# Constant products on TensorE in the waits of the router and of the last results, and a gather that begins with tile 0

## Chip, cores and metric

The kernel runs on one core of a Trainium2 chip. The metric is the device time of one execution in microseconds (us), and the median of several executions is compared.

## What is computed

A decoder trunk of two layers for one sequence of 256 tokens of width 1024, all float32. Each layer mixes tokens (layer 0 by causal pooling, layer 1 by attention with 16 heads), and then applies a mixture of experts: 32 experts in 4 groups, of which each token takes the best group and in it the best two experts. Cut to what matters here:

```python
for i in range(DEPTH):                                    # 2 layers
    h = rmsnorm(x, norm_mix_g[i]) * (1.0 + sc_m) + sh_m
    y = pool_mixer(...) if i % 2 == 0 else moba_attention(...)
    x = x + g_m * y
    h = rmsnorm(x, norm_ffn_g[i]) * (1.0 + sc_f) + sh_f
    x = x + g_f * hier_moe(h, ...)                        # 32 experts
return rmsnorm(x, final_norm_g)

# hier_moe: logits -> group, two experts e with weights combine[:, e]
for e in range(N_EXPERTS):
    he = jax.nn.silu(t @ w_gate[e]) * (t @ w_up[e])
    y = y + combine[:, e, None] * (he @ w_down[e])
```

sh, sc and g are six vectors per layer that come from the product of silu(c) with ada_w (1024 x 6144).

## The kernel before

The five engines run programs written out by hand, tied by semaphores. Nothing plans the order; what stands behind a waiting instruction on its engine waits too. SyncE (SP) issues all transfers of weights into `ring`, four slots of 3 MB (with a fifth slot `R` used once per layer), in a fixed order: an expert's gate and up weights are issued when its slot's `ring_free` comes (the slot's former gate and up have been used), its down weights at `down_free`.

The 256 tokens are two tiles (t = 0, 1) of 128. In each layer the mixture goes through these steps:

- `route(L)` on TensorE (PE): router logits, 16 transposes that bring x back to rows of tokens (line 557), the two small products of `strided`, and in layer 0 `part(7)`, a piece of silu(c) @ ada_w. Then it waits for `mask_ready`, the mask of chosen experts that VectorE (DVE) works out step by step. Five small products of 32 columns with the mask give the counts (`counts`), and `cols(7 + 8 * L)` does six products of one column each (128 x 1).
- From the counts DVE works out the place of each token among 512 places sorted by expert, and writes `pick[:, t, :]`, 128 x 512, of ones and zeros, in two instructions for each tile (lines 1542 and 1397; `pick_ready` rises after each tile).
- `gather(L)` on PE: for each of 8 blocks k of 128 features, two products over the tiles t into `bank[k % 4]` give the sorted tokens. It waits for both tiles of `pick`. ScalarE (ACT) moves each bank to `hS` (in `reg_a`, line 1094, `hS_ready`), and blocks 4 to 7 wait until the bank is free again.
- `first_hidden(L)` takes expert 0, then come the experts, 64 places each, in a rotation. Four times (`STAGES` and the end) `combine(L, s)` turns 128 finished places back to rows (8 transposes, line 726), waits until ACT and DVE have moved them to `yS` (line 1669 on DVE), and adds them into banks 4 to 7.
- `last_results(L)` ends the experts: the last transposes `turn_ye_of` (line 616), after which DVE writes the scaled result (line 1394), for which `combine(L, SB - 1)` waits.

All ordinary products stand at line 496 in the profile, in the helper `mm`. One float32 product of the program is two MATMUL instructions in the trace: a gather has 16 products and 32 instructions. In the names, `keep` holds `pick`, `reg_h` the tokens, `ye` the small arrays of the router, `cst` constants (the identity `ident` is its first 128 columns), `colp` and `colq` the vectors of the layer.

Of the kernel before, what the change touches and what calls it, by code (L numbers as in the profile page):

```python
# [11 lines left out]
T = SEQ // P  # L12
KC = D // P
NSLOT = SEQ * TOPK
SB = NSLOT // P
# [96 lines left out]
def program(nc, x, c, ada_w, ada_b, norm_mix_g, norm_ffn_g, pool_w, pool_scale, w_qkv, w_o,  # L112
# [3 lines left out]
    with ctx:  # L116
        def sb(name, shape, dt=F32):
            return ctx.enter_context(nc.sbuf_tensor(name, shape, dt))
# [3 lines left out]
        def S(*name):  # L122

            key = "_".join(map(str, name))
            if key not in sems:
                sems[key] = ctx.enter_context(nc.semaphore(key))
            return sems[key]
# [3 lines left out]
        cst = sb("cst", [P, NM])  # L131
        ident, tri = cst[:, 0:P], cst[:, P:2 * P]
# [47 lines left out]
        h_str = reg_h[:, :].rearrange("p (t k q) -> p t k q", t=T, k=KC)  # L180
# [3 lines left out]
        pick = keep[:, 0:T * NSLOT].rearrange("p (t s) -> p t s", t=T)  # L184
# [81 lines left out]
        bank = [ctx.enter_context(nc.psum_tensor(f"bank{i}", [P, 512], F32)) for i in range(8)]  # L266
# [10 lines left out]
        def cols_w(s, n):  # L277
            return ring[:, s, 0:KC * n].rearrange("p (k n) -> p k n", k=KC)
# [14 lines left out]
        def full_at(turn):  # L293

            return 16 * (turn + 1)
# [16 lines left out]
        def turn_bank(s, half):  # L312

            return bank[((STAGES + (0,))[s] + half) % 2]
# [17 lines left out]
        def lg_at(t, n):  # L332

            return bank[5][:, 384 + t * 64:384 + t * 64 + n]

        def cols_at(a):

            if a in (7, 15):
                return bank[4][:, 0:NB]
            return bank[7 if a < 8 else 6][:, NB * (a % 8):NB * (a % 8 + 1)]  # L340
# [153 lines left out]
        def _(pe):  # L494
            def mm(o_, l_, r_, start, stop):
                return nc.tensor.matmul(o_, l_, r_, start=start, stop=stop)  # L496

            def part(a, ready=None):

                s, turn = ADA_AT[a]  # L500
                w = cols_w(s, AC)
                if a:
                    pe.wait_ge(S("acc_act"), 2 * ADA_PE.index(a if ready is None else ready))
                for kk in range(2):
                    if kk == 0:
                        pe.wait_ge(S("ring_first", s), full_at(turn))
                    else:
                        pe.wait_ge(S("ring_mid", s), full_at(turn))
                        pe.wait_ge(S("ring_last", s), full_at(turn))
                    for b, (lo, hi) in enumerate(((0, 512), (512, AC))):  # L510
                        for g in range(4):
                            k = 4 * kk + g
                            last = mm(bank[part_bank[a][b]][32 * g:32 * g + 32, 0:hi - lo],
                                      cact[:, k:k + 1].broadcast_to([P, 32]), w[:, k, lo:hi], kk == 0, kk == 1)
                        if kk:
                            last.then_inc(S("part_full"), 1)

            def blocks(a, dst):

                one = quarter if a in ADA_PE else ones[:, 0:1]  # L520
                for j in range(NB):
                    if j in (0, 4):
                        pe.wait_ge(*acc_done(a, j // 4))
                    last = mm(dst[:, j:j + 1], acc_of(a)[:, j * P:(j + 1) * P], one, True, True)
                return last

            def cols(a):
                blocks(a, cols_at(a)).then_inc(S("cols_full"), 1)

            def strided(L):  # L530
# [3 lines left out]
                    last = mm(strided_at[:, i * KC:(i + 1) * KC], spread[:, i, :], in_eight, True, True)  # L534
                last.then_inc(S("strided_full"), 1)

            def squares(L, k):

                pe.wait_ge(S("sq_ready"), L * KC + max(k, 3) + 1)
                mm(bank[1][32 * (k % 4):32 * (k % 4) + 32, 0:SEQ], ones[:, 0:32], sqT[:, k, :], k < 4, k >= KC - 4)\  # L540
                    .then_inc(S("sums"), 1)
# [4 lines left out]
            def route(L):  # L546

                pe.wait_ge(S("L_kept"), L + 1)
                pe.wait_ge(S("S_kept"), L + 1)
                pe.wait_ge(S("bb_ready"), 1)  # L550
                for t in range(T):
                    mm(lg_at(t, NL), Lsb[:, t * P:(t + 1) * P], pull, True, True)
                    last = mm(lg_at(t, NL + 1)[:, NL:NL + 1], Ssb[:, t * P:(t + 1) * P], quarter, True, True)
                last.then_inc(S("lg_full"), 1)
                for t in range(T):
                    for k in range(KC):
                        last = nc.tensor.transpose(bank[2 * t + k // 4][:, k % 4 * P:(k % 4 + 1) * P],
                                                   xT[:, k, t * P:(t + 1) * P], ident)
                        if k % 4 == 3:
                            last.then_inc(S("x_back"), 1)  # L560
                pe.wait_ge(S("g_kept"), L + 1)
                strided(L)
                if L == 0:
                    part(7)
                pe.wait_ge(S("mask_ready"), L + 1)
                for t in range(T):
                    mm(bank[5][:, 0:E], ones[:, :], mask[:, t, :], t == 0, t == T - 1)
                mm(bank[5][:, E:2 * E], tri, mask[:, 0, :], True, True)
                mm(bank[5][:, 2 * E:3 * E], ones[:, :], mask[:, 0, :], True, False)
                mm(bank[5][:, 2 * E:3 * E], tri, mask[:, 1, :], False, True).then_inc(S("counts"), 1)  # L570
                cols(7 + 8 * L)

            def gather(L):

                pe.wait_ge(S("xr_ready"), 4 * L + 4)
                pe.wait_ge(S("x_kept"), 4 * L + 4)
                pe.wait_ge(S("pick_ready"), L * T + T)
                for k in range(KC):
                    if k >= 4:
                        pe.wait_ge(S("hS_ready"), L * KC + k - 3)  # L580
                    for t in range(T):
                        last = mm(bank[k % 4][:, :], h_str[:, t, k, :], pick[:, t, :], t == 0, t == T - 1)
                    last.then_inc(S("gathered"), 1)
# [71 lines left out]
            def turn_ye_of(L, e, b):  # L655

                pe.wait_ge(S("ye_ready", L), e + 1)
                turn_ye(bank[2 + b], b).then_inc(S("ye_turned", L), 1)
# [29 lines left out]
            def last_results(L):  # L688

                turn_ye_of(L, E - 2, 0)  # L690
                down_of(L, E - 1, *loaded(L, E - 1), 1)
                turn_ye_of(L, E - 1, 1)

            def overflow(L):

# [21 lines left out]
            def combine(L, s):  # L717

                if s == 0:
                    for half, t in by_tile:  # L720
                        mm(bank[4 + half + 2 * t][:, :], ident, x_sb[:, t, half * 512:half * 512 + 512], True, False)
                for half in range(2):
                    if half and s < SB - 1:
                        pe.wait_ge(S("heT_ready", L), STAGES[s] + 4)
                    for mq in range(4):
                        last = nc.tensor.transpose(turn_bank(s, half)[:, mq * P:(mq + 1) * P],  # L726
                                                   yT[:, half * 4 + mq, s * P:(s + 1) * P], ident)
                    last.then_inc(S("yT_turned"), 1)
                pe.wait_ge(S("yS_act"), SB * L + s + 1)
                pe.wait_ge(S("yS_dve"), SB * L + s + 1)  # L730
                for half, t in by_tile:
                    last = mm(bank[4 + half + 2 * t][:, :], pwT[:, s, t * P:(t + 1) * P],
                              yS[s][:, half * 512:half * 512 + 512], False, s == SB - 1)
                    if s == SB - 1:
                        last.then_inc(S("moe_out"), 1)
# [30 lines left out]
            for k in range(KC):  # L766
                for t in range(T):
                    last = nc.tensor.transpose(two(0, k)[:, t * P:(t + 1) * P], x_sb[:, t, k * P:(k + 1) * P], ident)  # L768
# [6 lines left out]
            for t in range(T):  # L775
                last = mm(bank[6][:, :], ones[:, :], band_sb[:, t, 0:2, :], t == 0, t == T - 1)
# [3 lines left out]
            for k in range(KC):  # L780
                for t in range(T):
                    last = mm(two(0, k), h[:, t, k * P:(k + 1) * P], band_sb[:, t, k // 2, :], t == 0, t == T - 1)
# [3 lines left out]
            for t in range(T):  # L786
                last = mm(bank[6][:, :], ones[:, :], band_sb[:, t, 2:4, :], t == 0, t == T - 1)
# [6 lines left out]
            for k in range(KC):  # L794
                pe.wait_ge(S("pT_ready"), 2 * (k // 2) + 2)
                for cc in range(2):
                    last = mm(mixed(0, k), pw[:, k // 2 * 2 + cc, k % 2 * P:(k % 2 + 1) * P], pT[:, k // 2 * 2 + cc, :],
                              cc == 0, cc == 1)
# [1092 lines left out]
```

## Time and profile before

| | |
|---|---|
| time, median of 3 (785.62, 787.03, 787.3) | 787.03 us |
| profiled execution: time, span | 786.15 us, 784.3 us |
| PE busy | 723.5 us, 92% of the span |
| DVE, ACT, POOL busy | 241.9, 170.1, 39.5 us |
| granted TensorE clock, mean | 0.972 |
| DMA, mean | 351 GB/s |

The profiled execution took 1.85 us more than the span from its first to its last instruction. PE is busy nearly throughout; its granted clock (PEclk) is 1.00 (2.4 GHz) or 0.50 (1.2 GHz). Times within the trace are from the start of the span.

### The profile page before, as it was taken

Reading aid. Unit: us, or ns where it says so; the run is one execution under the profiler, and the core shown is the slowest. Engines: PE = TensorE matmul, PEld = TensorE weight load, DVE = VectorE, ACT = ScalarE, POOL = GpSimd, SP = SyncE. Lnnn points to the kernel's source line nnn. Section 1 sums busy time; section 2 is a strip of 40 time slices with the busy share of each in tenths; the row PEclk is TensorE's granted clock in tenths of the full one; section 3 lists DMA queues with packets and bytes.
Section 4 is the critical chain, followed back from the end, with each engine's and each line's share of the span. In section 5 each row is a group of like instructions: output and inputs, shape, how many; then the busy total and the mean of one; then the engine's idle time right before and its main releaser. Section 6 shows DMA issues by size and latency. Waiting matters only on the chain.

```text
span 784.3 us, 12427 instructions
## 1 busy us (share of the span) xinstructions
PE 723.5 (92%) x4568; PEld 430.2 (55%) x4568; DVE 241.9 (31%) x660; ACT 170.1 (22%) x394; POOL 39.5 (5%) x71
## 2 busy tenths in 40 slices
PE   4988699999989999979999999969999998999995
PEld 2664545555544445426888888744555554454542
DVE  0113515111211211153777553261511221121113
ACT  4112441111110111142123232244111111011113
POOL 0000000000100000000000000000000100000000
PEclk9989799999999999997999999979999999999999
DMA  8999999999999999999796755182999999999961
GB/s 342 396 400 391 412 367 377 386 418 415 420 415 417 417 416 418 403 391 331 298 378 239 237 196 232 64 333 99 386 384 422 417 417 417 416 419 414 418 246 56
DMA packets 70451, 274.93 MB, mean 351 GB/s; under 512 B 4480, under 2 KB 17920, under 8 KB 53888
## 3 DMA queue, kind: packets, MB, share of 16 engines
q1 hardware_dynamic: 70400, 274.23, 88.3%
q8 instruction: 34, 0.56, 0.3%
q14 instruction: 17, 0.14, 0.0%
HBM read 273.16 MB, written 1.05 MB: 350 GB/s over the span
## 4 chain that ended last, share of the span: by engine, by line
PE 83%; DMA 9%; DVE 3%; issue 2%; SPq 1%; ACT 1%; DVEq 0%; ACTq 0%
PE bank L496 74%; DMA ring<-in_exp_w_up_dram 5%; PE bank L616 4%; DMA ring<-in_ada_w_dram 4%; PE bank L603 2%; PE bank L726 1%; SPq L361 1%; PE bank L909 1%; DVE ye L1394 1%; PE bank L768 0%; DVE keep L1397 0%; DVE reg_h L1669 0%; DVE keep L1669 0%; DVE reg_a L1397 0%; ACT ye L1049 0%
## 5 line engine op out<-in xcount | busy, mean ns | idle before, releaser
L496 PE MATMUL bank<-ring,xe 128*64 128x256 f32 x1984 | 227.8, 382 | 6.6 <-DMA ring<-in_exp_w_up_dram 6.1
L496 PEld LDWEIGHTS bank<-ring,xe 128*64 128x64 f32 x1984 | 139.6, 137 | 78.3 <-issue 12.1
L496 PE MATMUL bank<-ring,heT 128*64 128x512 f32 x512 | 123.9, 604 | 0.0
L1394 DVE TENSOR_TENSOR reg_c<-reg_c,bank 128x128 f32<-128x128 f32 x64 | 18.5, 288 | 279.6 <-ACT reg_c L1113 279.6
L468 POOL COPY xe<-reg_a 128x512 f32 x62 | 38.1, 614 | 689.0 <-PE bank L496 368.1
L1049 ACT ACTIVATE ye<-bank 128x512 f32<-128x512 f32 (+1 forms) x72 | 41.7, 585 | 139.1 <-PE bank L496 138.9
L1113 ACT ACTIVATE reg_c<-bank 128x128 f32<-128x128 f32 x64 | 17.8, 278 | 241.1 <-PE bank L496 238.6
L496 PE MATMUL bank<-reg_b,ring 128*128 128x256 f32 x256 | 60.9, 393 | 1.7 <-ACT reg_b L1258 1.7
L1394 DVE TENSOR_TENSOR reg_b<-bank,colp 128x512 f32 x64 | 44.3, 692 | 43.3 <-issue 35.8
L496 PEld LDWEIGHTS bank<-ring,heT 128*64 128x64 f32 x512 | 31.2, 136 | 47.3 <-issue 47.0
L496 PEld LDWEIGHTS bank<-reg_b,ring 128*128 128x128 f32 x256 | 49.5, 197 | 8.9 <-issue 2.2
L496 PE MATMUL bank<-ring,cact 128*32 128x512 f32 (+1 forms) x320 | 32.8, 548 | 19.5 <-DMA ring<-in_ada_w_dram 16.9
L616 PE MATMUL bank<-cst,ye 128*128 128x128 f32 x256 | 41.9, 286 | 2.9 <-ACT ye L1049 2.9
L1397 DVE SCALAR_TENSOR_TENSOR ring<-ring,cact 128x768 f32<-128x768 f32 x42 | 42.7, 1017 | 1.2
L616 PEld LDWEIGHTS bank<-cst,ye 128*128 128x128 f32 x256 | 26.7, 140 | 28.1 <-issue 23.1
L496 PE MATMUL bank<-reg_a,ring 128*128 128x256 f32 x160 | 39.2, 405 | 2.2 <-DVE reg_a L1397 1.5
L496 PE MATMUL bank<-keep,reg_h 128*128 128x512 f32 x64 | 33.6, 691 | 4.4 <-DVE keep L1397 4.4
L603 PEld LDWEIGHTS bank<-cst,reg_c 128*128 128x128 f32 x64 | 8.9, 138 | 50.5 <-issue 48.7
L496 PEld LDWEIGHTS bank<-reg_a,ring 128*128 128x128 f32 x160 | 32.0, 204 | 8.3 <-issue 2.1
L496 PEld LDWEIGHTS bank<-ring,cact 128*32 128x32 f32 x320 | 10.3, 118 | 39.2 <-issue 38.1
L1637 DVE COPY heT<-bank 128x128 f32<-128x128 f32 x64 | 18.7, 292 | 42.3 <-PE bank L603 42.3
L496 PE MATMUL bank<-ring,reg_b 128*128 128x256 f32 x128 | 29.8, 386 | 0.0
(165 smaller groups left out, 543.5 us busy)
## 6 DMA issues: line engine op xcount, KB each, us to landing
ring<-in_exp_w_gate_dram SPq DMA_DIRECT2D x64, 1024.0 KB, 13.6
ring<-in_exp_w_up_dram SPq DMA_DIRECT2D x64, 1024.0 KB, 15.6
ring<-in_exp_w_down_dram SPq DMA_DIRECT2D x64, 1024.0 KB, 12.7
ring<-in_ada_w_dram SPq DMA_DIRECT2D x16, 1536.0 KB, 12.3
ring<-in_ada_w_dram SPq DMA_DIRECT2D x32, 768.0 KB, 12.4
ring<-in_w_qkv_dram SPq DMA_DIRECT2D x12, 1024.0 KB, 12.3
ring<-in_w_o_dram SPq DMA_DIRECT2D x4, 768.0 KB, 7.5
x_sb<-in_x_dram SPq DMA_DIRECT2D x1, 1024.0 KB, 5.1
```

What stands on the lines that cost most here:

```text
L361: sp.dma_start(dst[:, a:b], src[:, a:b]).then_inc(S(name, s), 16)
L468: nc.gpsimd.tensor_copy(xe[:, b, :, :], hS[:, :, bass.ds(off, CAP)]).then_inc(S("xe_ready", L), 1)
L496: return nc.tensor.matmul(o_, l_, r_, start=start, stop=stop)
L603: return nc.tensor.transpose(dst[:, 2 * P:3 * P], he[:, b, :], ident)
L616: last = nc.tensor.transpose(dst[:, cq * P:(cq + 1) * P], ye[:, b, cq * P:(cq + 1) * P], ident)
L726: last = nc.tensor.transpose(turn_bank(s, half)[:, mq * P:(mq + 1) * P], yT[:, half * 4 + mq, s * P:(s + 1) * P], ident)
L909: last = nc.tensor.transpose(bank[5 + a][:, s * P:(s + 1) * P], sc[m % 2][a][:, s * P:(s + 1) * P], ident)
L1049: return nc.scalar.activation(o_, i_, ACT.Identity)
L1113: nc.scalar.activation(sil[:, b, :], bank[b][:, 0:P], ACT.Silu).then_inc(S("sil_ready", L), 1)
L1394: return nc.vector.tensor_tensor(o_, a_, b_, op)
L1397: return nc.vector.scalar_tensor_tensor(o_, a_, s_, b_, op0, op1)
L1637: nc.vector.tensor_copy(heT[:, b, :], bank[b][:, 2 * P:3 * P]).then_inc(S("heT_ready", L), 1)
```

## The change

A new helper `keep_busy(n, b)` on PE issues n products of the identity with the first 512 columns of `cst`, which never change, into bank b. Nothing reads their result. It is called in five kinds of places: in `route`, before the wait for the mask (4 products, layer 1 alone) and after `cols` (1 in layer 0, 3 in layer 1), at the end of `last_results` (1), and in the last `combine` between the transposes and the wait for `yS` (1). And `gather` does tile 0 of blocks 0 to 3 as soon as tile 0 of `pick` is there, then tile 1 of these blocks; blocks 4 to 7 are as before. No other engine's program is changed.

```diff
+            def keep_busy(n, b):
+
+                for i in range(n):
+                    mm(bank[b][:, :], ident, cst[:, 0:512], True, True)
+
...
                 strided(L)
                 if L == 0:
                     part(7)
+                else:
+                    keep_busy(4, 6)
                 pe.wait_ge(S("mask_ready"), L + 1)
...
                 cols(7 + 8 * L)
+                keep_busy(3 if L else 1, 6)
 
             def gather(L):
 
                 pe.wait_ge(S("xr_ready"), 4 * L + 4)
                 pe.wait_ge(S("x_kept"), 4 * L + 4)
-                pe.wait_ge(S("pick_ready"), L * T + T)
-                for k in range(KC):
-                    if k >= 4:
-                        pe.wait_ge(S("hS_ready"), L * KC + k - 3)
+                for t in range(T):
+                    pe.wait_ge(S("pick_ready"), L * T + t + 1)
+                    for k in range(4):
+                        last = mm(bank[k][:, :], h_str[:, t, k, :], pick[:, t, :], t == 0, t == T - 1)
+                        if t == T - 1:
+                            last.then_inc(S("gathered"), 1)
+                for k in range(4, KC):
+                    pe.wait_ge(S("hS_ready"), L * KC + k - 3)
                     for t in range(T):
                         last = mm(bank[k % 4][:, :], h_str[:, t, k, :], pick[:, t, :], t == 0, t == T - 1)
                     last.then_inc(S("gathered"), 1)
...
                 turn_ye_of(L, E - 1, 1)
+                keep_busy(1, 0)
...
                     last.then_inc(S("yT_turned"), 1)
+                if s == SB - 1:
+                    keep_busy(1, 2)
                 pe.wait_ge(S("yS_act"), SB * L + s + 1)
```

On PE in layer 0, between `cols(7)` (the products of 128x1) and the gather, the order with its waits changes so; `cst` alone is the constant product:

```order
 L496 MATMUL bank<-cst,ring 128x1 [waits acc_act]
 L496 MATMUL bank<-cst,ring 128x1
+L496 MATMUL bank<-cst 128x512
 L496 MATMUL bank<-keep,reg_h 128x512 [waits pick_ready,x_kept,xr_ready]
-L496 MATMUL bank<-keep,reg_h 128x512 x7
+L496 MATMUL bank<-keep,reg_h 128x512 x3
+L496 MATMUL bank<-keep,reg_h 128x512 [waits pick_ready]
+L496 MATMUL bank<-keep,reg_h 128x512 x3
 L496 MATMUL bank<-keep,reg_h 128x512 [waits hS_ready]
```

One product is put ahead of the gather, and the eight products of blocks 0 to 3 are split into four for tile 0 and four that wait for tile 1.

On PE in layer 1, from `strided` (128x8) to the products with the mask (`ye`), the order changes so:

```order
 L496 MATMUL bank<-cst,ring 128x8 [waits spread_ready,g_kept]
 L496 MATMUL bank<-cst,ring 128x8
+L496 MATMUL bank<-cst 128x512 x4
 L496 MATMUL bank<-ye,ones 128x32 [waits mask_ready]
 L496 MATMUL bank<-ye,ones 128x32
```

Four products stand ahead of the wait for the mask. Three more stand behind `cols(15)`, where layer 0 has one; the gather is split in the same way.

On PE at the end of a layer, from the last `turn_ye_of` (line 616, now 628) to the last products of `combine`:

```order
-L616 MATMUL bank<-cst,ye 128x128 [waits ye_ready_0]
-L616 MATMUL bank<-cst,ye 128x128 x3
-L752 COMPARE_AND_BRANCH [waits dn_free_0]
-L726 MATMUL bank<-cst,reg_b 128x128 x8
+L628 MATMUL bank<-cst,ye 128x128 [waits ye_ready_0]
+L628 MATMUL bank<-cst,ye 128x128 x3
+L496 MATMUL bank<-cst 128x512
+L767 COMPARE_AND_BRANCH [waits dn_free_0]
+L739 MATMUL bank<-cst,reg_b 128x128 x8
+L496 MATMUL bank<-cst 128x512
 L496 MATMUL bank<-reg_h,reg_c 128x512 [waits yS_dve,yS_act]
```

One product stands ahead of each of the two waits.

## Rows read from the trace of the kernel before

**Rows 1.** The page: the span, and PE's clock in 40 slices.

```profile
span 784.3 us, 12427 instructions
...
PEclk9989799999999999997999999979999999999999
```

**Rows 2.** Chain that ended last, in order of time: start, length (us), what.

```profile
93.51 0.75 DVE keep L1397
...
95.59 20.61 PE bank L496 x64
...
212.30 21.29 DMA ring<-in_exp_w_up_dram
...
524.39 0.75 DVE keep L1397
...
526.47 20.21 PE bank L496 x64
```

**Rows 3.** Windows: stretch, length, busy by engine (instructions), PEclk, DMA share, GB/s.

```profile
88.05:93.40 5.35, 5.34 (x30) 4.77 (x22) 2.21 (x10) 2.54 (x5) 0.00 (x0) 0.50 1.02 416
95.59:101.70 6.11, 6.11 (x8) 2.50 (x9) 4.86 (x13) 0.78 (x1) 0.00 (x0) 0.50 1.01 414
351.16:354.28 3.12, 3.12 (x20) 1.10 (x24) 2.69 (x6) 0.98 (x2) 0.00 (x0) 0.50 1.09 348
360.10:364.50 4.40, 4.14 (x38) 4.04 (x36) 0.17 (x1) 0.00 (x0) 0.00 (x0) 1.00 1.07 358
366.25:371.36 5.11, 5.11 (x12) 4.12 (x13) 0.80 (x3) 2.25 (x4) 0.00 (x0) 0.50 1.07 379
516.70:521.50 4.80, 1.09 (x11) 1.08 (x10) 3.27 (x22) 4.78 (x8) 0.00 (x0) 1.00 1.00 412
521.56:524.28 2.72, 2.72 (x14) 2.63 (x13) 2.21 (x10) 0.91 (x3) 0.00 (x0) 0.50 0.17 63
526.47:531.79 5.32, 5.32 (x7) 2.22 (x8) 4.79 (x13) 0.78 (x1) 0.00 (x0) 0.50 0.99 416
770.20:774.93 4.73, 1.77 (x15) 1.30 (x13) 1.39 (x2) 1.85 (x3) 0.00 (x0) 1.00 0.01 2
```

**Rows 4.** Timeline of weight loads in layer 0's gather: start, length, what.

```profile
96.58 0.34 PEld L496 LDWEIGHTS bank<-keep,reg_h 128*128 128x128 f32 x1 [0.52 <-issue]
...
100.84 0.34 PEld L496 LDWEIGHTS bank<-keep,reg_h 128*128 128x128 f32 x1 [0.52 <-issue]
...
102.14 0.19 PEld L496 LDWEIGHTS bank<-keep,reg_h 128*128 128x128 f32 x1 [0.24 <-issue]
...
111.58 0.19 PEld L496 LDWEIGHTS bank<-keep,reg_h 128*128 128x128 f32 x1 [0.24 <-issue]
```

**Rows 5.** Timeline: products of one column, a bank moved by ACT, the first hidden products.

```profile
57.60 1.47 PE L496 MATMUL bank<-cst,ring 128*128 128x1 f32 x12 [0.38 <-ACT ring L1049]
...
102.33 0.78 ACT L1094 ACTIVATE reg_a<-bank,colq 128x512 f32<-128x512 f32 x1 [2.11 <-PE bank L496]
...
112.53 3.67 PE L496 MATMUL bank<-ring,reg_a 128*64 128x256 f32 x32
...
521.58 2.70 PE L496 MATMUL bank<-ones,ring 128*128 128x1 f32 x12
...
543.01 3.67 PE L496 MATMUL bank<-ring,reg_a 128*64 128x256 f32 x32
```

**Rows 6.** Timeline of PE at the end of layer 1.

```profile
772.97 1.08 PE L726 MATMUL bank<-cst,reg_b 128*128 128x128 f32 x8 [0.99 <-DVE reg_b L1394]
...
774.93 3.67 PE L496 MATMUL bank<-reg_h,reg_c 128*128 128x512 f32 x8 [0.88 <-DVE reg_h L1669]
```

**Rows 7.** Windows again, for the DMA share; and a row of the waits.

```profile
114.00:119.00 5.00, 5.00 (x47) 3.32 (x45) 1.64 (x9) 2.44 (x5) 0.86 (x2) 1.00 0.52 179
...
534.00:546.00 12.00, 12.00 (x50) 5.76 (x50) 0.00 (x0) 6.15 (x8) 0.61 (x1) 1.00 0.00 0
...
PE bank L496 <- DMA ring<-in_exp_w_up_dram: 6.1, 5, 1.6
```

## The prediction

> **What bounds the kernel now.** I read the page first. The span is 784.3 us, and PE's clock is below 9 (90% of full speed) in only four of the 40 slices; two of these are the fifth (78 to 98 us) and the twenty-seventh (510 to 529 us) [rows 1]. There the two routers lie. The chain that ended last comes second: through both routers it goes over DVE's writing of `pick` and then straight into PE, from 95.59 for 20.61 us in layer 0 and from 526.47 for 20.21 us in layer 1, which is the gather and expert 0 [rows 2]. So whatever makes the gathers end earlier moves the first expert. Third, the windows, for the clock: layer 0's gather runs at 0.50 (1.2 GHz) for its first 6.11 us, layer 1's for 5.32 us [rows 3]. Last, DMA, since the experts' weights could hold the experts back: PE waits for up weights 6.1 us in five places [rows 7], so the gain must also get through the stream of weights.
>
> A gather is 32 instructions. The weight loads ahead of them give the pace of PE: 5 steps from 96.58 to 100.84 at the low clock, 0.852 us each; 22 steps from 102.14 to 111.58 at the high one, 0.429 us each [rows 4]. Check on before, layer 0: 6.11 us at 0.852 do 7.2 instructions, the other 24.8 take 10.65 us, and 95.59 + 6.11 + 10.65 = 112.35; the first hidden product stands at 112.53 [rows 5], 0.18 later. Layer 1 by the same sum: 526.47 + 5.32 + 25.8 x 0.429 = 542.84, against 543.01 [rows 5]. I add 0.18 below.
>
> **How the clock behaves here.** Four stretches begin with dense products at the low clock, and it rose 6.11, 3.12, 5.11 and 5.32 us later [rows 3]; the mean is 4.9. Small products do not raise it: from 88.05 to 93.40 PE was busy 5.34 of 5.35 us with products of 32 columns and of one, and the clock was 0.50 throughout [rows 3]. Nor do they hold it: over 4.14 busy us up to 364.50, nearly all of one column, it was 1.00, and the next dense stretch began at 0.50 [rows 3]. In layer 1 it outlasted an almost empty stretch from 516.70 and fell at 521.56, in the midst of such small products [rows 3]. A page of the Trainium skill says why such times differ: TensorE: Matmul & The Clock Gate, section Part 1, has the phase of the clock's control run free of the kernel, so that the number of slow products changes from run to run. This trace agrees so far as its four rises took 3.12 to 6.11 us.
>
> **The change in layer 0.** Up to `cols(7)` nothing moves: PE ends its small products at about 93.3. Then one constant product, two instructions at 0.852, goes to 95.0. Tile 0 of `pick` is written at 93.51 + 0.75 = 94.26 [rows 2], so the gather now starts at 95.0 and not at 95.59; the constant product eats 0.6 us of the 1.2 us that the split gives. The eight instructions for tile 0 last beyond 98, long after tile 1 is there. Dense work now begins at 93.3. With the mean of 4.9 us at the low clock, 5.8 of 34 instructions are slow and 28.2 take 12.1 us: 93.3 + 4.9 + 12.1 + 0.18 = 110.5. That is 2.0 us earlier than 112.53; with the ends of the rows, 3.12 and 6.11, it is 2.9 and 1.4.
>
> **Does this reach the end of the layer?** PE does an expert faster than the weights come, and catches up with them: the chain goes over an up transfer from 212.30 for 21.29 us [rows 2]. The stream of weights must therefore move as well. Expert 0's hidden products free a slot of the ring, and meanwhile DMA runs dry: a share of 0.52 over 114 to 119 is 2.4 us idle [rows 7]. The slot comes 2.0 us earlier, and up to 2.4 us can be taken back there. I count all 2.0. In layer 1 DMA is wholly idle from 534 to 546 [rows 7]; its restart hangs on expert 0 alone, and the gain there goes through whole.
>
> **The change in layer 1.** Four constant products are 8 instructions, 3.43 us at 0.429. They start behind `strided` at 516.7, where the clock is 1.00 [rows 3], and end at 520.15, ahead of the mask's products at 520.4; they cost nothing while the clock is high. They fill most of the stretch whose emptiness went before the fall at 521.56. If the clock stays up, the 12 one-column instructions take 1.47 us as at 57.60, not 2.70 as at 521.58 [rows 5], and end at 523.05. The three constant products take 6 x 0.429 = 2.57, to 525.6. Tile 0 of `pick` is ready at 524.39 + 0.75 = 525.14 [rows 2], so the constant products, not `pick`, set the start, 0.9 us before 526.47. All 32 instructions at 0.429 are 13.73: 525.6 + 13.73 + 0.18 = 539.5, against 543.01: 3.5 us. ACT moves a bank in 0.78 us [rows 5], within the 0.86 us of two instructions, so the banks come free in time.
>
> **The ends of the layers.** The two waits before line 726 and before the last products are 0.99 and 0.88 us long [rows 6]; a constant product at 0.429 is 0.86. Both fit with 0.1 and 0.02 us to spare. At the low clock it would be 1.70 and each wait would be 0.8 longer, but the clock here was 1.00 [rows 3]. The last eight instructions ran at full pace already, 3.67 us [rows 6], so I see no gain; I take 0.1 us of loss in all, between 0 and 0.4.
>
> **Sum.** 2.0 + 3.5 - 0.1 = 5.4 us. The profiled execution took 786.15 us, which gives 780.75. The three timed ones lie 0.5 us above it on the mean (786.65) and 0.9 on the median; as the clock's moods differ from run to run I add half the 0.5: 781.0 us, 0.8% below 787.03.
>
> **Rivals.**
> - The clock falls in layer 1 all the same, because the small products from 520.4 to 523 lie in between; the run up to 364.50 speaks for it, the fact that these are shorter (2.6 us) against it. Then the dense work from 523.05 on begins low: 4.9 us with 5.8 instructions, the other 32.2 of 38 in 13.8, end at 541.95. Layer 1 gains 1.1 (0.5 to 1.9), the whole 3.0: 783.4 us. 24%.
> - The stream of weights keeps its pace in layer 0 and PE merely waits longer for it in that stretch: then the 2.0 are lost, 783.0 us. The idle DMA of [rows 7] speaks against it. 8%.
> - The four products meet a low clock in layer 1: 8 x 0.852 = 6.8 us from 516.7, the mask's products 3.1 late, and all behind them. The clock is then high for the gather, which ends at 542.6: layer 1 gains 0.4, together 784.1 us. 3%.
> - The other side: constant products do not raise or hold the clock at all. Layer 0 then only starts 0.6 earlier. In layer 1 the clock falls at 521.56 as before, the one-column products end at 524.28, and 6 x 0.852 = 5.1 us of constant products hold the gather back to 529.4, 2.9 us later than before; it then has its own 5.32 us at the low clock. Net 2.3 + 0.1 slower: 788.8 us. This decides as soon as the three products run low with the gather cold behind them; even two (3.4 us) would hold the gather back by 1.2. Against it: their shape is that of the gather's own products, which raised the clock twice. 5%. Near this stands a sentence of the Trainium skill, TensorE: Matmul & The Clock Gate, section Part 4: a transpose, which is a product with the identity, does not count as busy for the clock in the same way. If it held for ordinary products with the identity, this case would be the outcome. In the trace even real transposes did not bring the clock down: 770.20 to 774.93 holds only 1.77 busy us, nearly all transposes, and stands at 1.00 [rows 3].
>
> **How the numbers follow.** The forecast has 58%; 2% are left for what I do not see. From 781.0, the bounds of layer 0 alone are -0.9 and +0.6, the ends of the layers +0.3, and the first three rivals reach 784.1. The range is 779.5 to 784.3. A measurement of this kernel can tell about 0.2%, 1.6 us: faster by more than that holds in the forecast and the first three rivals, 92%; within it 3%, slower 5%.
>
> **What would show it.** In the changed trace: the clock back at 1.00 some 5 us after 93.3; no stretch at 0.50 between 520 and 540; one-column products of layer 1 in 1.47 us; the mask's products still at 520.4 minus the gain of layer 0; the gathers' first hidden products near 110.5 and, with layer 0's 2.0 taken off, 537.5; a shorter idle time of DMA behind 114; longer waits for up weights only by tenths. The prediction is wrong if the clock is low in layer 1's gather, or if the time gained at 110 is gone at 340.

## The result

The changed kernel takes 779.53 us in the median of six executions (777.39 to 780.42), the kernel before 786.9 us (783.25 to 788.58): a ratio of 0.9909 with a 95% interval of 0.9883 to 0.9935, 7.2 us faster and between 5.1 and 9.2. Timed again in a later job it gave 0.9921 (0.9889 to 0.9952). The forecast, 781.0 us, is a ratio of 0.9923 to the 787.03 on record before it; both intervals hold it. The profiled executions took 786.15 and 780.42 us, so the traces have to explain 5.7 us. The changed kernel's profiled execution is the longest of its six.

The page of the changed kernel: the span, PE's busy time and clock.

```profile
span 778.6 us, 12475 instructions
...
PE 730.6 (94%) x4592; PEld 432.1 (55%) x4592; DVE 242.0 (31%) x660; ACT 169.9 (22%) x394; POOL 39.5 (5%) x71
...
PEclk9999699999999999998999999999999999999999
```

With the 24 new MATMUL instructions PE's busy time is 7.1 us longer, while the span is 5.7 us shorter: PE is idle for 48.0 us instead of 60.8, so the new work lies in what was idle. The slice of layer 1's router, the twenty-seventh, no longer dips as in [rows 1]; the fifth, of layer 0, still does.

The chain that ended last, in order of time: start, length, what.

```profile
92.31 0.76 DVE keep L1412
93.08 0.14 issue
93.21 19.27 PE bank L496 x64
...
208.58 21.32 DMA ring<-in_exp_w_up_dram
...
516.42 24.33 PE bank L496 x92
```

In layer 0 the chain still goes over `pick`, but over that of tile 0. The stretch of DMA begins 3.72 us earlier than in [rows 2] and is as long as before: the weights moved with the gather. In layer 1 the chain does not touch `pick` any more. PE is the chain from the mask on, with the constant products in it.

PE's timeline in both routers, from the mask's products (`ye`) to the first hidden products (64x256 on `reg_a`):

```profile
88.38 0.63 PE L496 MATMUL bank<-ye,ones 128*128 128x32 f32 x4
...
89.52 1.48 PE L496 MATMUL bank<-cst,ring 128*128 128x1 f32 x12
90.86 1.11 PE L496 MATMUL bank<-cst 128*128 128x512 f32 x2
93.21 15.67 PE L496 MATMUL bank<-keep,reg_h 128*128 128x512 f32 x32 [1.25 <-DVE keep L1412]
108.81 3.67 PE L496 MATMUL bank<-ring,reg_a 128*64 128x256 f32 x32
...
512.56 3.68 PE L496 MATMUL bank<-cst 128*128 128x512 f32 x8
516.42 0.63 PE L496 MATMUL bank<-ye,ones 128*128 128x32 f32 x4 [0.17 <-DVE ye L1409]
...
517.56 1.48 PE L496 MATMUL bank<-ones,ring 128*128 128x1 f32 x12
518.90 4.45 PE L496 MATMUL bank<-cst 128*128 128x512 f32 x6
523.14 14.01 PE L496 MATMUL bank<-keep,reg_h 128*128 128x512 f32 x32
537.08 3.67 PE L496 MATMUL bank<-ring,reg_a 128*64 128x256 f32 x32
```

And the windows that answer to [rows 3] and [rows 7]:

```profile
76.20:86.44 10.24, 9.69 (x48) 7.20 (x48) 4.97 (x30) 4.80 (x7) 0.00 (x0) 0.50 1.04 407
86.44:93.28 6.84, 5.59 (x53) 3.46 (x45) 3.53 (x14) 3.78 (x8) 0.00 (x0) 1.00 1.02 416
93.28:96.68 3.40, 3.40 (x4) 1.34 (x5) 3.12 (x10) 0.00 (x0) 0.00 (x0) 0.50 1.00 414
512.56:519.94 7.38, 7.21 (x35) 4.47 (x35) 5.32 (x32) 5.95 (x10) 0.00 (x0) 1.00 0.72 294
519.94:523.36 3.42, 3.42 (x6) 1.36 (x5) 3.17 (x10) 0.00 (x0) 0.00 (x0) 0.50 0.95 340
110.00:115.00 5.00, 5.00 (x47) 3.33 (x45) 1.43 (x7) 2.72 (x5) 1.15 (x2) 1.00 1.01 409
117.00:122.00 5.00, 5.00 (x39) 2.54 (x37) 3.22 (x21) 0.87 (x2) 0.61 (x1) 1.00 0.90 334
```

Layer 0, 3.72 us earlier at its first hidden product (108.81 against 112.53 in [rows 5]). Of these, 0.16 were there before the mask. The mask's products took 1.14 us up to the one-column products, where they had taken 2.15 (88.54 to 90.69) in the trace of before, since the clock had come back at 86.44. That is 1.01, and no edit stands ahead of it. From the one-column products to the gather it was 3.69 us instead of 4.90: 1.21, the head start of tile 0, whole. The gather itself took 15.60 instead of 16.94: 1.34, as its low stretch was 3.4 us long and not 6.11. Whether that is the change's doing is asked below.

Layer 1, from the mask to the first hidden product: 20.66 us (516.42 to 537.08) instead of 22.59 (520.42 to 543.01), 1.93 us. The four products cost nothing: the mask's products begin 4.22 us behind those of `strided`, as before (512.20 to 516.42, 516.20 to 520.42). But the clock fell at 519.94, in the midst of the three: 4.45 us for what takes 2.82 in a later trace of the kernel, and the gather begins 0.7 us later behind the one-column products than before. It then runs at the high clock nearly throughout, 13.94 us instead of 16.54.

The rest: DMA no longer runs dry right behind the gather of layer 0 (1.01 where [rows 7] has 0.52). From there to layer 1's mask 0.28 us more were gained: `part(9)` met the high clock (2.79 us for its first 32 instructions, which took 4.31 before), and most of that was lost again in layer 1's mixing, 0.88 of it in a wait for ACT at 389. Another 0.2 us were lost among the experts of layer 1.

### The profile page after: what moved, and what is told of

Its sections match the earlier page's. It is cut to its first block, busy times and chain, and to the rows that moved or that the text cites. A ratio compares the mean times of both kernels' runs of the same rounds, so it can differ in the third digit from the quotient of the medians.

```text
span 778.6 us, 12475 instructions
## 1 busy us (share of the span) xinstructions
PE 730.6 (94%) x4592; PEld 432.1 (55%) x4592; DVE 242.0 (31%) x660; ACT 169.9 (22%) x394; POOL 39.5 (5%) x71
## 3 DMA queue, kind: packets, MB, share of 16 engines
HBM read 273.16 MB, written 1.05 MB: 352 GB/s over the span
## 4 chain that ended last, share of the span: by engine, by line
PE 80%; DMA 10%; DVE 5%; SPq 2%; issue 1%; ACT 1%; DVEq 0%; ACTq 0%
PE bank L496 71%; DMA ring<-in_exp_w_up_dram 5%; PE bank L628 4%; DMA ring<-in_ada_w_dram 4%; DVE ring L1412 2%; PE bank L615 2%; PE bank L739 1%; SPq L361 1%; PE bank L924 1%; SPq L373 0%; PE bank L562 0%; PE bank L783 0%; DVE ye L1409 0%; DVE keep L1684 0%; DVE reg_a L1412 0%
## 5 line engine op out<-in xcount | busy, mean ns | idle before, releaser
L496 PE MATMUL bank<-keep,reg_h 128*128 128x512 f32 x64 | 29.7, 624 | 1.2 <-DVE keep L1412 1.2
```

## The experiments

The kernels of one job stand beside runs of the kernel before on the same chip. As the clock's low stretches differ between executions of one kernel, two numbers are read of each: the ratio, over 6 to 12 executions, and in its trace the length from the mask's products to the first hidden product, called layer 0's or layer 1's stretch below (23.99 and 22.59 us before, 20.43 and 20.66 in the changed trace). A trace is one execution and need not be a typical one: those of the first three kernels below are among the shortest of their twelve (780.27, 781.26 and 781.51 us).

### The parts alone, and products that are busy but narrow

All diffs here are against the changed kernel. `e1_split_alone` has no constant product at all:

```diff
-                else:
-                    keep_busy(4, 6)
...
-                keep_busy(3 if L else 1, 6)
...
-                keep_busy(1, 0)
...
-                if s == SB - 1:
-                    keep_busy(1, 2)
```

`e2_route_alone` has those of the router, without the last two `keep_busy` of that diff and with the gather of before; `e3_ends_alone` has the last two and not the first two, again with

```diff
-                for t in range(T):
-                    pe.wait_ge(S("pick_ready"), L * T + t + 1)
-                    for k in range(4):
...
+                pe.wait_ge(S("pick_ready"), L * T + T)
+                for k in range(KC):
+                    if k >= 4:
+                        pe.wait_ge(S("hS_ready"), L * KC + k - 3)
```

`e4_one_column` has the whole change with

```diff
-                for i in range(n):
-                    mm(bank[b][:, :], ident, cst[:, 0:512], True, True)
+                for i in range(7 * n // 2):
+                    mm(bank[b][:, 0:1], ident, cst[:, 0:1], True, True)
```

> The change's gather (tile 0 of blocks 0 to 3 first) without any constant product. Clock theory (the gain is mostly the clock, held or raised by constant products): the gathers start 1.2 us earlier in each layer, still at the low clock for 3 to 6 us; 1.2 to 2.4 us faster than before, some 785. Rival, head start theory (the gain of 7.4 us is mostly the earlier start): 5 us or more faster, 782 or less.

> The constant products of the router alone (4 before the mask and 3 behind the one-column products in layer 1, 1 in layer 0); the gather waits for both tiles as before, and none at the ends of the layers. Clock theory: 4 to 5.5 us faster than before, some 782, with the low clock ending within about 3 us of the start of the gathers. Head start theory: within 1.5 us of before.

> Only the constant product at the end of last_results and the one in the last combine. Clock theory as predicted: nothing to gain, as the clock is high there; 0 to 0.4 us slower, within 1 us of before. Rival, ends theory (in unprofiled executions the clock often falls at the ends of the layers, 3.4 us lost in each, and this is where the 2 us lie that the sum did not have): 1.5 us or more faster.

> The whole change, but each constant product of 512 columns is replaced by 3.5 products of one column, which keep PE busy for as long (some 0.86 us at the high clock). Clock theory, with dense columns as what counts: the low stretches of before come back, and the time is that of the split alone, 784 to 787. Rival (any busy PE holds the clock): as the changed kernel, 779.5.

| kernel | median us (before 786.2) | ratio, 95% | stretch of layer 0, 1 (us) |
|---|---|---|---|
| split alone | 782.47 | 0.9953 (0.9932 to 0.9975) | 20.43, 22.76 |
| router's products alone | 783.13 | 0.9963 (0.9941 to 0.9984) | 21.47, 19.92 |
| ends alone | 785.07 | 0.9981 (0.9962 to 0.9999) | 21.48, 22.61 |
| one column | 785.31 | 0.9981 (0.9960 to 1.0002) | 21.44, 25.91 |

The three ratios multiply to 0.9897, close to the whole change's 0.9909: within these intervals the parts add up. Each interval leaves out 1, that of the ends only just. The split gave 3.7 us (2.0 to 5.3) where 1.2 to 2.4 were expected, a miss upward, though the interval reaches into what was expected; in its trace layer 0's stretch is 3.6 us shorter and layer 1's 0.2 longer. Most of the 3.6 is not the split's. The ends alone leave the router and the gather of layer 0 as they were, and their trace has this:

```profile
87.89 0.63 PE L496 MATMUL bank<-ye,ones 128*128 128x32 f32 x4
...
93.90 15.54 PE L496 MATMUL bank<-keep,reg_h 128*128 128x512 f32 x32 [3.40 <-DVE keep L1405]
109.37 3.67 PE L496 MATMUL bank<-ring,reg_a 128*64 128x256 f32 x32
```

Here too the clock was high when the mask came, and the stretch is 21.48 us, 2.51 shorter than 23.99 without any edit in it. So at the same clock the split alone is worth 1.05 us in layer 0, its head start. What more it gave in the ratio no trace shows. The router's products gave 2.9 us (1.3 to 4.6), less than the 4 to 5.5 expected, but they made layer 1's stretch 2.7 us shorter. The ends gave 1.5 (0.1 to 3.0), where a loss of 0 to 0.4 was expected; what they may save is seen by accident in the trace of the router's products alone. Its windows at the end of layer 1:

```profile
758.00:766.10 8.10, 5.49 (x30) 2.27 (x27) 2.37 (x4) 1.19 (x2) 0.00 (x0) 1.00 0.00 1
766.10:772.92 6.82, 5.95 (x12) 2.79 (x11) 0.85 (x2) 3.62 (x8) 0.00 (x0) 0.50 0.02 5
```

and its timeline there:

```profile
763.94 0.66 PE L624 MATMUL bank<-cst,ye 128*128 128x128 f32 x4 [1.09 <-ACT ye L1057]
765.59 1.51 PE L734 MATMUL bank<-cst,reg_b 128*128 128x128 f32 x8 [0.99 <-DVE reg_b L1402]
767.98 6.12 PE L496 MATMUL bank<-reg_h,reg_c 128*128 128x512 f32 x8 [0.87 <-DVE reg_h L1677]
```

Without products in these waits the clock can fall there: the last eight instructions took 6.12 us, not 3.67 as in [rows 6], and from the last `turn_ye_of` to the end of the span it was 15.46 us, against 12.98 in the trace of before and 13.01 in the changed one. Four kernels have no product there (`before`, `e1_split_alone`, `e2_route_alone`, `e9_no_ends`), and their traces hold eight ends of a layer: in two of them, this one and layer 0's in `e1_split_alone`, the last eight instructions were slow. In the nine traces with the wide products they were so in none of 18.

The narrow products keep PE as busy. Layer 1 in the trace of `e4_one_column`, first PE's timeline, then two windows:

```profile
511.79 4.21 PE L496 MATMUL bank<-cst 128*128 128x1 f32 x28
515.86 1.04 PE L496 MATMUL bank<-ye,ones 128*128 128x32 f32 x4
...
517.99 2.70 PE L496 MATMUL bank<-ones,ring 128*128 128x1 f32 x12
520.55 4.41 PE L496 MATMUL bank<-cst 128*128 128x1 f32 x20
524.82 17.03 PE L496 MATMUL bank<-keep,reg_h 128*128 128x512 f32 x32
541.77 3.46 PE L496 MATMUL bank<-ring,reg_a 128*64 128x256 f32 x30
```

```profile
511.80:515.86 4.06, 4.06 (x31) 4.06 (x30) 3.40 (x22) 4.06 (x7) 0.00 (x0) 0.76 1.00 407
513.90:530.96 17.06, 17.06 (x61) 13.45 (x61) 10.73 (x38) 3.81 (x8) 0.00 (x0) 0.50 0.67 264
```

PE is busy without a gap from 511.8 on, and the clock falls at 513.90 all the same and stays low for 17.06 us, until the gather is 6.1 us old. The stretch is 25.91 us, 3.3 longer than before. The gather begins 8.96 us behind the mask's products instead of 6.05, 2.9 later, as the rival on the other side had it for constant products that neither raise nor hold the clock; 0.97 of this is in the mask's products themselves, as the fall came earlier than that rival assumed. So in this trace a PE that was busy throughout with one-column products neither kept the clock from falling nor brought it back; with the wide products in the same places it stayed at 1.00 in five of six traces (below). The median, 785.31, lies in the 784 to 787 expected; whether the kernel is slower than the split alone (0.9981 against 0.9953) their intervals leave open.

### Which of layer 1's products, and the order of the small ones

`e5_no_first_four` and `e6_no_three` each drop one place:

```diff
-                else:
-                    keep_busy(4, 6)
```

```diff
-                keep_busy(3 if L else 1, 6)
+                if L == 0:
+                    keep_busy(1, 6)
```

`e7_cols_early` is

```diff
                 strided(L)
                 if L == 0:
                     part(7)
                 else:
-                    keep_busy(4, 6)
+                    cols(15)
+                    keep_busy(3, 6)
                 pe.wait_ge(S("mask_ready"), L + 1)
...
-                cols(7 + 8 * L)
-                keep_busy(3 if L else 1, 6)
+                if L == 0:
+                    cols(7)
+                keep_busy(4 if L else 1, 6)
```

and `e8_changed_again` is the changed kernel.

> The changed kernel without the four constant products ahead of the mask in layer 1. Theory (they keep the clock up over the mask's and the one-column products, and so the three behind short): the clock falls before the mask as in the kernel before, the three products run at 0.852 an instruction and hold the gather back by some 2 us: about 2 us slower than the changed kernel. Rival (the three alone, right ahead of the gather, are what matters): within 0.5 us of the changed kernel.

> The changed kernel without the three constant products behind the one-column products in layer 1 (the one of layer 0 stays). Theory: the clock, held until the mask, falls before or in the gather, which loses 1.5 to 2.4 us at the low clock but starts with tile 0 at once: about 1.5 us slower than the changed kernel. Rival (the three cost as much as they give, as in the trace where they took 4.45 us and held the gather back): within 0.5 us, or faster.

> The changed kernel with the one-column products of layer 1 moved ahead of the wait for the mask, followed by three constant products, and four constant products behind the mask's products. Theory (the clock fell at 519.94 in the changed trace because mask's and one-column products stand together): no low stretch in layer 1's router or gather, the first hidden product there 1.5 to 2 us earlier than in the changed trace, 778 us. Rival (the fall comes whatever the order): within 0.5 us of the changed kernel.

> The changed kernel itself, for a comparison on the same chip: 7.2 us faster than before within 1 us, 779.5, and a second trace of it. Whether layer 1's low stretch comes again is open: by the theory it hangs on the phase of the clock's control, by a rival it comes at the same instruction each time.

| kernel | median us (before 785.61) | ratio, 95% | stretch of layer 0, 1 (us) |
|---|---|---|---|
| without the first four | 782.85 | 0.9969 (0.9945 to 0.9993) | 18.73, 22.31 |
| without the three | 780.09 | 0.9936 (0.9911 to 0.9960) | 18.74, 21.40 |
| one-column products early | 779.46 | 0.9940 (0.9912 to 0.9968) | 21.41, 18.63 |
| changed, again | 780.45 | 0.9921 (0.9889 to 0.9952) | 21.20, 18.96 |

The changed kernel's second trace has no low stretch in layer 1:

```profile
518.95 2.82 PE L496 MATMUL bank<-cst 128*128 128x512 f32 x6
521.61 13.90 PE L496 MATMUL bank<-keep,reg_h 128*128 128x512 f32 x32
535.44 3.67 PE L496 MATMUL bank<-ring,reg_a 128*64 128x256 f32 x32
```

The three products take 2.66 us to the gather, the gather 13.83, the stretch 18.96: 3.63 us shorter than before, for which the forecast had 3.5. So the fall in the first trace came not from the instruction but from the moment. Without the first four the clock fell at 517.10, behind the mask's products:

```profile
516.87 2.51 PE L496 MATMUL bank<-ones,ring 128*128 128x1 f32 x12
519.24 5.14 PE L496 MATMUL bank<-cst 128*128 128x512 f32 x6
524.21 13.90 PE L496 MATMUL bank<-keep,reg_h 128*128 128x512 f32 x32
```

The three hold the gather back: 4.97 us up to it, where the second changed trace has 2.66: of the 3.35 us by which its way from the mask's products to the gather is longer (8.48 against 5.13), they make 2.3 and the slow one-column products 1.0. The gather itself is as fast as can be. Expected were 2 us over the changed kernel; the ratio says 3.8, the medians 2.4, with intervals of the ratios that just overlap. Without the three, the gather begins on time and takes 16.57 us, with the clock low from 517.18 to 524.00; its stretch is 2.4 longer than the 18.96, but the ratio (0.9936) cannot be told from the changed kernel's. Over all jobs, the last one below included, eleven traces have the wide products of layer 1 in their two places or lack them. Where either place is empty the clock fell ahead of the gather in all five: at 521.56 before, 512.84 in `e1_split_alone`, 516.90 in `e3_ends_alone`, 517.10 and 517.18 here. Where the four and the three both stand, `e2_route_alone` included, it fell in one of six.

The early one-column products give what the trace was to show, no low stretch from 510 to 534 and 0.33 us less than 18.96, and nothing that the times can tell: the expected 1.5 us is missed, because it was reckoned against the one trace in which the fall had come.

### The ends, layer 0, and a combination

`e9_no_ends` is the changed kernel without the two products at the ends (the last two `keep_busy` of the first diff above). `e10_no_layer0` and `e11_ends_doubled` are

```diff
-                keep_busy(3 if L else 1, 6)
+                if L:
+                    keep_busy(3, 6)
```

```diff
-                keep_busy(1, 0)
+                keep_busy(2, 0)
...
-                    keep_busy(1, 2)
+                    keep_busy(2, 2)
```

and `e12_cols_early_two` is `e7_cols_early` with `keep_busy(4 if L else 2, 6)` behind the columns.

> The changed kernel without the constant products at the ends of the layers (the router's and the split stay). As predicted: the ends give nothing, so the time is that of the changed kernel or 0.1 us less, some 0.992 of before. Ends theory, from the trace of the router's products alone, where the clock fell at 766.10 and the stretch from the last transposes to the end took 2.5 us longer: an execution in some pays 2.5 us at the end of layer 1, so on the mean 0.5 to 1.5 us slower than the changed kernel, 0.993 to 0.994 of before.

> The changed kernel without the one constant product behind cols(7) in layer 0. As predicted (it lets the clock rise earlier but eats 0.6 us of the head start): 0.5 to 1 us slower than the changed kernel. Rival (layer 0 lives from the split alone, as its stretch from mask to first hidden product was 20.43 us with and without the product): no difference beyond 0.3 us.

> The changed kernel with two constant products in place of one at each of the two waits at the ends of the layers. If one product just fills its wait, the second lies on the path: in the trace, last products of layer 1 begin 1.5 to 1.7 us later behind the last turn_ye_of, while in layer 0 part(9) begins no later, since 2.6 us of slack lie ahead of it; 1.6 us slower than the changed kernel. Rival (the products are off the path, done in time): no difference.

> One-column products of layer 1 ahead of the mask with three and four constant products around it, as before, and two constant products in place of one in layer 0. Theory (dense products right up to the gather are what shortens or spares the low stretch): layer 1 without a low stretch, layer 0's gather low for less long; 1 us faster than the changed kernel on the mean, 0.991 of before. Rival (where the clock is low already, the second product costs 1.7 us of the head start in layer 0): 0.5 to 1 us slower than with one.

| kernel | median us (before 788.48) | ratio, 95% | stretch of layer 0, 1 (us) |
|---|---|---|---|
| without the ends | 779.96 | 0.9911 (0.9878 to 0.9943) | 21.66, 18.96 |
| without layer 0's | 779.48 | 0.9887 (0.9862 to 0.9912) | 20.36, 18.96 |
| ends doubled | 780.3 | 0.9919 (0.9887 to 0.9951) | 20.39, 18.96 |
| early, two in layer 0 | 780.81 | 0.9910 (0.9881 to 0.9939) | 18.74, 18.63 |

These ratios lie within 0.35% of each other and of the changed kernel's, on six executions each; the differences of 0.5 to 1.6 us that were expected cannot be seen in them. What the traces show is firmer. The doubled ends, at the end of layer 1:

```profile
763.86 0.65 PE L628 MATMUL bank<-cst,ye 128*128 128x128 f32 x4 [1.09 <-ACT ye L1064]
764.35 1.88 PE L496 MATMUL bank<-cst 128*128 128x512 f32 x4
766.07 1.04 PE L739 MATMUL bank<-cst,reg_b 128*128 128x128 f32 x8
766.95 1.88 PE L496 MATMUL bank<-cst 128*128 128x512 f32 x4
768.66 3.60 PE L496 MATMUL bank<-reg_h,reg_c 128*128 128x512 f32 x8
```

The last products begin 4.80 us behind the last `turn_ye_of`; with one product in each wait it was 3.61 (765.59 to 769.20) in the changed kernel, the same as before. So one product costs 0.00 us there and the second 0.6 at each place, 1.2 at this end where 1.5 to 1.7 were expected; at layer 0's end, up to `part(9)`, it is 0.5 where none was expected.

The trace without the ends shows, by chance, the layer 0 that the forecast had reckoned with, the clock low from 87.34 on:

```profile
88.48 1.06 PE L496 MATMUL bank<-ye,ones 128*128 128x32 f32 x4
...
90.64 2.70 PE L496 MATMUL bank<-cst,ring 128*128 128x1 f32 x12
93.20 2.05 PE L496 MATMUL bank<-cst 128*128 128x512 f32 x2
95.05 15.16 PE L496 MATMUL bank<-keep,reg_h 128*128 128x512 f32 x32
110.14 2.16 PE L496 MATMUL bank<-ring,reg_a 128*64 128x256 f32 x18
```

The constant product delays the gather to 95.05 (95.0 in the forecast), and the first hidden product stands at 110.14 (110.5). Without layer 0's product the gather started at 95.33 by tile 0 alone, and the stretch was 20.36 us, no longer than the 20.43 with it. The seven traces with the split and one product spread from 18.73 to 21.66: in two of them (`e5_no_first_four`, `e6_no_three`) layer 0's gather had no low stretch at all, in neither of the two with the split and no product (20.43, 20.36). That may be its gain or chance; the time shows none (0.9887 without it). Two products in layer 0 fitted before `pick` when the clock was high (93.07 to 95.03, gather at 95.43) and the gather there had no low stretch, but the time shows nothing of it. No version is shown to be faster than the changed kernel.

## Why the prediction was right

**The whole.** Both the direction and the size came out: 5.4 us from the sum, 5.7 in the pair of traces, 6 as forecast for the median, 7.2 (5.1 to 9.2) measured. The measured median, 779.53, is just inside the range, whose lower end is 779.5; the bounds given for layer 0 reach down to 780.1 only, and the 0.6 below that came from no term, so that it lies inside is luck. The chances of the forecast and the first three rivals add up to 93%, not 92. The parts of the sum were less well met in the one changed trace than their total, since the clock fell at other moments in it.

**Layer 0, 2.0 us.** The mechanism was right, and its working holds to 0.4 us in a trace where the clock is as before (95.05 and 110.14). There the stretch is 21.66, 2.3 shorter than before. In the changed trace the gain was 3.7. There 1.01 came from small products that happened to meet the high clock, and the head start of tile 0 came whole, 1.21, because the constant product ran in 1.1 us and not in 1.7 and ended before `pick`. The kernel with the gather and router of before has the same luck in `e3_ends_alone`: 21.48 instead of 23.99. So of the 3.56 us by which the stretch is shorter 2.51 are luck and 1.05 the change's. What failed is the step that took one trace's clock at 88 us for the kernel's. Depending on the clock the change is worth 1.05 to 2.3 us here, with the forecast's 2.0 between. Of that the split is the part that is shown; that the constant product adds to it is not.

**Layer 1, 3.5 us.** Right where the clock stays up: 3.63 in the second changed trace, and 18.96 us again in three further traces with the same router of layer 1 (`e9_no_ends`, `e10_no_layer0`, `e11_ends_doubled`). The first changed trace is the first rival, forecast at 1.1 (0.5 to 1.9) and measured at 1.93: the fall was not before the three products, as reckoned, but in them. So one of five traces shows the fall, one of six with `e2_route_alone`, for a chance of 24% given to it. That the four products cost nothing is right (516.42 against 512.56 + 3.43).

**Does it reach the end of the layer.** Yes: the DMA stretch of the chain moved by 3.72 us, the same as the first hidden product, though 2.4 us was all I had counted as recoverable over 114 to 119. A second idle time from 122 to 126 (share 0.75, now 0.87 over the same work) gave another 0.5; where the other 0.8 come from I can't place. At `part(9)` 3.70 us are still there (347.46 against 351.16), so the time gained at 110 was not gone at 340. PE's wait for up weights in layer 0 stayed at three of about 1.1 us.

**The ends, 0.1 us of loss and no gain.** Half wrong. The loss is 0.00, as each product fits its wait. No gain was argued from one trace in which the clock had stayed high there; in `e2_route_alone` it fell and the end took 2.5 us longer, and the ends alone gave a ratio of 0.9981 (0.9962 to 0.9999). But the changed kernel without them gave 0.9911 (0.9878 to 0.9943) beside 0.9909 and 0.9921 with them, so that they gain is likely and not shown. The remark on transposes from the Trainium skill, TensorE: Matmul & The Clock Gate, section Part 4, pointed at this place, and I set it aside on one trace. The traces do not agree about it: over the two groups of transposes at layer 1's end the clock stayed at 1.00 in `before`, `e1_split_alone` and `e9_no_ends`, and in `e2_route_alone` it fell in the second. At layer 0's end a low clock costs little: in `e1_split_alone` the last eight instructions took 6.46 us, and `part(9)` began 10.10 us behind the last `turn_ye_of`, against 9.95 before, since PE has 2.66 us of idle time there in any case.

**The rivals.** The rival that the weights absorb layer 0's gain fell. The four products at a low clock were seen in no trace. That constant products do not hold the clock is refuted for wide ones: with both places filled it stayed up in five of six traces, and fell in all five without. For one-column products layer 1 of `e4_one_column` shows the held-back gather of that rival; over its executions the kernel is not slower than before (0.9981, 0.9960 to 1.0002).

What stays open: how the 1.5 us between the sum of the traces and the median is shared out, within the interval; why the split alone gave 3.7 us where its trace shows 1.05 at the same clock; and whether layer 0's product and those of the ends are worth anything.

## What to carry to other kernels

Where an engine's queue has an idle stretch of some microseconds ahead of wide float32 products, constant products of the same width in just that stretch are free and can keep the following ones at 0.43 instead of 0.85 us an instruction; here they did so in five of six traces. Their number is best chosen so that they end before what is waited for even at the low clock (the advice follows from the 4.45 us of the three, no run tries it). Read the clock from more than one trace before its low stretches enter a sum: here the same code gave 18.96 or 20.66 us in layer 1, and layer 0 untouched 23.99 or 21.48. And start a long chain of products with the half of its operand that is ready first: that needs no added work and alone gave 0.9953 (0.9932 to 0.9975), which can't be told from the router's constant products (0.9963).

## What was not expected of the hardware

PE 100% busy is no sign of a high clock: with one-column products, each with its full weight load, it was busy for all of 17.06 us at 1.2 GHz, the last 6.1 of them with wide products (`e4_one_column`, 513.90 to 530.96). Twelve one-column instructions took 1.34 us at the high clock (89.52 to 90.86 in the changed trace) and 2.56 at the low one (90.64 to 93.20 in `e9_no_ends`), 0.11 and 0.21 each, so they too slow down.
